# Gate and up products of four feed-forwards as seven block products instead of eight, with weight sums made by VectorE and by accumulating DMAs

## The chip, the cores and the metric

One NeuronCore of one Trainium2 chip. The metric is the device time of the kernel in microseconds (us). The kernel before took 2505.16 us (median of three runs, 2500.97 to 2505.35). TensorE is called PE, VectorE DVE, ScalarE ACT, GpSimd POOL and SyncE SP, as in the profile; PEld is PE's weight load.

## The reference, cut to what matters

A token block `x` of 512 tokens by 1024 features passes a first block (attention, short convolution, an expert feed-forward) and then a second block of two layers. Each layer of the second block holds two dense feed-forwards, so there are four, in this order: before and after a pooling mixer, before and after a latent attention.

```python
D_FF = 2816
FFN_HALF = 0.5

def swiglu(h, w_gate, w_up, w_down):
    return (jax.nn.silu(h @ w_gate) * (h @ w_up)) @ w_down

for i in range(DEPTH_2):
    h = rmsnorm_2(x, ffn1_norm[i])
    x = x + FFN_HALF * swiglu(h, ffn1_w_gate[i], ffn1_w_up[i], ffn1_w_down[i])
    h = rmsnorm_2(x, mix_norm[i])
    ...
    h = rmsnorm_2(x, ffn2_norm[i])
    x = x + FFN_HALF * swiglu(h, ffn2_w_gate[i], ffn2_w_up[i], ffn2_w_down[i])
```

All values are float32. The change touches `h @ w_gate` and `h @ w_up` alone.

## The kernel before

Features lie on the 128 partitions and tokens along the free dimension, so `x` is 8 tiles (`KD`) of 128x512. A feed-forward has 22 inner tiles (`KF`) of 128 features each. For one inner tile the kernel loads a strip of the gate weights and a strip of the up weights (128x1024 each, 512 KB), and later 16 strips of the down weights (128x1408). Each of the 88 gate, 88 up and 64 down strips goes the same way. SP loads it into one of four slots of `stage` (`strip`). ACT copies it as fp32r to `wH` (`hi`, L699). DVE writes what the copy left out to `wL` (`lo`, L1856). PE then makes three products for each 128x128 weight tile (`three`, L1142 to L1144): high by high, high by low and low by high, with the split activations `hH` and `hL`. A gate or up strip is 8 x 3 = 24 matmuls of 512 columns, an inner tile 48 and a pair of inner tiles 96. `wH` and `wL` have two slots, so `hi(n)` waits until strip n-2 has been used.

An inner tile (`inner` in `ffn`) takes two banks of PSUM, and successive tiles alternate between two pairs of banks. DVE multiplies the gate bank by `rstd` into `hraw` (L2355) and the up bank into `gf` (L2358), which frees the banks (`out_taken`). ACT takes silu of `hraw` (L739), DVE multiplies (L2361), ACT copies to `gH` (L742) and DVE writes `gL` (L2364). The normalisation factor `rstd` is made while the first two tiles are multiplied; it is applied to the products, not to their input. The down products read `gH` and `gL`, and DVE adds half of each into `x` (L2406).

Each engine runs its own queue in program order, and semaphores tie them. In each feed-forward DVE's queue is: `lo` of strips 2 and 3, the reciprocal (L1871), `lo` of strip 4, `inner(0)`, `lo` of strip 5, `inner(1)`, and then always two strips and one tile. The mixer of the first layer has products of 256 columns (`token_product`, 96 matmuls by `three`), the only ones in the trace with fp32r operands that read split weights as the moving side at 256 columns.

Of the kernel before, what the change touches and what calls it, by code (L numbers as in the profile page):

```python
# [134 lines left out]
def build(nc, A, out):  # L135
    st = ExitStack()
    with st:
# [22 lines left out]
        hL = place("hL", [P, KD, T], F32R, HL)  # L160
        stage = place("stage", [P, STAGE, WIDE], F32, ST)
        wH = place("wH", [P, 2, WIDE], F32R, WH)
        wL = place("wL", [P, 2, WIDE], F32R, WL)
# [81 lines left out]
        gH = place("gH", [P, KF, T], F32R, G)  # L245
        gL = place("gL", [P, KF, T], F32R, G + KF * TILE)

        tok = place("tok", [P, NB, D], F32, G)
        band = place("band", [P, NBAND], F32, G + 37 * KB)
        zero = place("zero", [1, P + T], F32R, G + 42 * KB)  # L250
        squares2 = place("squares2", [P, KD, T], F32, G + 56 * KB)
# [86 lines left out]
        pos_loaded, angle, sines = sem("pos_loaded"), sem("angle"), sem("sines")  # L338
# [4 lines left out]
        out_stored = sem("out_stored")  # L343
# [4 lines left out]
        NFFN = 2 * KF + 2 * KD  # L348
        POOL = FFN1A + NFFN
        FFN2A = POOL + 4  # L350
        FFN1B = FFN2A + NFFN
        M_IN = FFN1B + NFFN
# [5 lines left out]
        N_STRIPS = FFN2B + NFFN  # L358
        width = [KD * P] * FFN1A
        ffn_width = [KD * P] * (2 * KF) + [WIDE] * (2 * KD)  # L360
        width += ffn_width + [4 * P] * 4 + ffn_width + ffn_width
        width += [KD * P] * 11 + [KQ * P] * 12 + [KD * P] * 2 + [KD * P] * KD + ffn_width
# [3 lines left out]
        T_POOL = T_FFN1A + KF + KD  # L366
        T_FFN2A = T_POOL + KD
        T_FFN1B = T_FFN2A + KF + KD
        T_MIN = T_FFN1B + KF + KD
# [52 lines left out]
        def halves(n):  # L422

            if FFN1A <= n < FFN1A + 2:
                return firstH[:, n - FFN1A, :], firstL[:, n - FFN1A, :]
            return wH[:, n % 2, 0:width[n]], wL[:, n % 2, 0:width[n]]
# [52 lines left out]

        block = st.enter_context(nc.Block())  # L480
# [3 lines left out]
        def _(sp):  # L484
# [19 lines left out]
            def ffn_tiles(n0, f, it):  # L504
                for j in range(2):
                    g = j if it is None else it * 2 + j
                    strip(n0 + 2 * j, A["gate"][f][g], it)
                    strip(n0 + 2 * j + 1, A["up"][f][g], it)

            def ffn(n0, f, start=0):  # L510
                down = A["down"][f]
                with sp.Fori(start, KF // 2) as i:
                    ffn_tiles(n0, f, i)
# [172 lines left out]
        def _(act):  # L686
# [49 lines left out]
            def ffn(n0, t0, f, q):  # L736
# [24 lines left out]
                if f:  # L761
                    hi(n0 + 5)
# [1964 lines left out]
```

## Time and profile before

| what | value |
|---|---|
| three runs | 2505.35, 2500.97, 2505.16 us |
| span of the profiled execution | 2501.0 us |
| PE busy | 2458.6 us, 98% of the span |
| DVE busy | 1132.8 us, 45% |
| ACT busy | 735.2 us, 29% |
| POOL busy | 49.5 us, 2% |
| DMA | 404.29 MB, mean 162 GB/s |
| granted clock of PE | mean 0.994 of full |

The profile has no time of its own for the profiled execution beside its span. The span is 4.2 us below the median of the runs and equal to the fastest of them within 0.1 us.

The feed-forwards lie at 740 to 1124 us, 1149 to 1509 us, 1509 to 1870 us and 2137 to 2501 us. In the profile a matmul's duration overlaps that of the next one, so the pace is read from starts, not from durations.

### The profile page before, as it was taken

The numbers are of one execution on the slowest core, as the hardware profiler recorded it, in microseconds if no ns is written. First come the engines' busy times: TensorE is split into PE (matmuls) and PEld (weight loads), VectorE is DVE, ScalarE is ACT, GpSimd is POOL, SyncE is SP. The second block draws the span as 40 slices with busy tenths as digits, with TensorE's granted clock in tenths as the row PEclk, the third lists the DMA queues.
The fourth block names the chain that finished last, engine by engine and source line by source line (L and its number), as shares of the span: only waits on it lengthen the run. The fifth ranks groups of instructions, "written<-read, shape, count | busy, mean of one in ns | idle before, by whom it ended". The sixth has DMA issues, their size and how long they took to land.

```text
span 2501.0 us, 29717 instructions
## 1 busy us (share of the span) xinstructions
PE 2458.6 (98%) x11265; PEld 1802.0 (72%) x11265; DVE 1132.8 (45%) x1732; ACT 735.2 (29%) x1049; POOL 49.5 (2%) x28
## 2 busy tenths in 40 slices
PE   7999999999999999999999999999999999999999
PEld 4876744434437888888888888888887667888887
DVE  6785312222227444336444334444337565544422
ACT  4245210100014333224333223333224354333321
POOL 0042000000000000000000000000000000000000
PEclk8999999999999999999999999999999999999999
DMA  7552699999992223313222322323222211223332
GB/s 309 191 168 98 262 408 421 421 420 421 421 407 89 98 94 112 102 55 110 92 100 99 104 91 84 101 92 113 96 90 68 80 43 43 93 92 101 105 104 68
DMA packets 84654, 404.29 MB, mean 162 GB/s; under 512 B 9176, under 2 KB 9560, under 8 KB 60896
## 3 DMA queue, kind: packets, MB, share of 16 engines
q1 hardware_dynamic: 84576, 403.22, 43.3%
q8 instruction: 53, 0.87, 0.1%
q14 instruction: 25, 0.20, 0.0%
HBM read 401.08 MB, written 2.10 MB: 161 GB/s over the span
## 4 chain that ended last, share of the span: by engine, by line
PE 92%; DVE 4%; ACT 2%; DMA 1%; issue 1%; SPq 0%; ACTq 0%; DVEq 0%
PE pair L1142 23%; PE pair L1144 23%; PE pair L1143 23%; PE pair L1438 9%; PE pair L1463 4%; PE pair L1374 2%; PE pair L1693 1%; PE pair L1831 1%; PE pair L1402 1%; PE pair L1288 1%; PE pair L1801 1%; PE pair L1802 1%; DMA ada_first<-in_w_ada 1%; PE pair L1403 1%; DMA stage<-in_gate 0%
## 5 line engine op out<-in xcount | busy, mean ns | idle before, releaser
L1856 DVE TENSOR_TENSOR wL<-stage,wH 128x1024 fp32r<-128x1024 f32 (+3 forms) x301 | 389.0, 1292 | 775.0 <-ACT wH L699 774.5
L1142 PE MATMUL pair<-hH,wH 128*128 128x512 f32 x1672 | 658.4, 394 | 8.5 <-DVE hL L1966 2.9
L1144 PE MATMUL pair<-hH,wL 128*128 128x512 f32 x1672 | 651.7, 390 | 0.0
L1143 PE MATMUL pair<-hL,wH 128*128 128x512 f32 x1672 | 651.6, 390 | 0.0
L699 ACT ACTIVATE wH<-stage 128x1024 fp32r<-128x1024 f32 (+3 forms) x301 | 335.2, 1114 | 842.1 <-PE pair L1144 842.1
L1142 PEld LDWEIGHTS pair<-hH,wH 128*128 128x128 f32 x1672 | 314.4, 188 | 80.3 <-DVE hL L1901 4.2
L1143 PEld LDWEIGHTS pair<-hL,wH 128*128 128x128 f32 x1672 | 314.5, 188 | 66.9 <-issue 2.4
L1144 PEld LDWEIGHTS pair<-hH,wL 128*128 128x128 f32 x1672 | 314.4, 188 | 65.8
L1142 PE MATMUL pair<-gH,wH 128*128 128x512 f32 x704 | 273.9, 389 | 0.0
L1143 PE MATMUL pair<-gL,wH 128*128 128x512 f32 x704 | 273.9, 389 | 0.0
L1144 PE MATMUL pair<-gH,wL 128*128 128x512 f32 x704 | 273.9, 389 | 0.0
L1438 PE MATMUL pair<-ring,xsT 128*64 128x512 f32 x1008 | 225.0, 596 | 0.0
L1438 PEld LDWEIGHTS pair<-ring,xsT 128*64 128x64 f32 x1008 | 69.3, 137 | 135.6 <-issue 134.9
L1142 PEld LDWEIGHTS pair<-gH,wH 128*128 128x128 f32 x704 | 132.1, 188 | 27.6
L1144 PEld LDWEIGHTS pair<-gH,wL 128*128 128x128 f32 x704 | 132.1, 188 | 27.5
L1143 PEld LDWEIGHTS pair<-gL,wH 128*128 128x128 f32 x704 | 132.1, 188 | 27.2
L1463 PE MATMUL pair<-ring,hidT 128*64 128x512 f32 x448 | 101.6, 607 | 6.0 <-issue 4.4
L2257 DVE SCALAR_TENSOR_TENSOR x<-pair,mod,x 128x512 f32<-128x512 f32 x64 | 45.5, 747 | 135.7 <-PE pair L1403 135.7
L739 ACT ACTIVATE sg<-hraw 128x512 f32<-128x512 f32 x88 | 55.7, 633 | 167.1 <-DVE hraw L2355 167.1
L2364 DVE TENSOR_TENSOR gL<-gf,gH 128x512 f32 (+1 forms) x88 | 61.0, 693 | 77.5 <-ACT gH L742 77.5
L1463 PEld LDWEIGHTS pair<-ring,hidT 128*64 128x64 f32 x448 | 31.6, 139 | 66.4 <-issue 64.0
L742 ACT ACTIVATE gH<-gf 128x512 f32 (+1 forms) x88 | 55.7, 633 | 76.7 <-DVE gf L2361 76.7
(365 smaller groups left out, 2135.1 us busy)
## 6 DMA issues: line engine op xcount, KB each, us to landing
ring<-in_experts SPq DMA_DIRECT2D x182, 1024.0 KB, 19.5
stage<-in_gate SPq DMA_DIRECT2D x88, 512.0 KB, 3.2
stage<-in_up SPq DMA_DIRECT2D x88, 512.0 KB, 3.2
stage<-in_down SPq DMA_DIRECT2D x64, 704.0 KB, 4.0
adaw<-in_w_ada SPq DMA_DIRECT2D x32, 512.0 KB, 5.2
stage<-in_w_in SPq DMA_DIRECT2D x18, 512.0 KB, 3.7
ring<-in_experts SPq DMA_DIRECT2D x16, 512.0 KB, 11.4
stage<-in_mla_in SPq DMA_DIRECT2D x9, 512.0 KB, 3.3
```

The costliest lines, as they stand in the source:

```text
L699: act.activation(halves(n)[0], stage[:, n % STAGE, 0:width[n]], ACT.Copy).then_inc(strip_hi, 1)
L739: act.activation(sg[:, tile % 2, :], hraw[:, tile % 2, :], ACT.Silu).then_inc(silu_done, 1)
L742: act.activation(dst, gf[:, tile % 2, :], ACT.Copy).then_inc(g_hi, 1)
L1142: pe.matmul(ps, lh, rh, start=first, stop=False)
L1143: pe.matmul(ps, lh, rl, start=False, stop=False)
L1144: return pe.matmul(ps, ll, rh, start=False, stop=last)
L1374: mm = pe.matmul(ps, xt[:, i, k * P:(k + 1) * P], pick[:, i, :], start=(i == 0), stop=(i == NB - 1))
L1438: mm = pe.matmul(pb[2 * g + half][64 * j:64 * j + 64, :], xsT[:, k, 64 * j:64 * j + 64], w[j][:, half * 512:(half + 1) * 512], start=(k == ...
L1463: mm = pe.matmul(pb[4 + half][64 * j:64 * j + 64, :], hidT[:, k, 64 * j:64 * j + 64], w[j][:, half * 512:(half + 1) * 512], start=(k == 0) ...
L1856: dve.tensor_tensor(low, stage[:, n % STAGE, 0:w], high, ALU.subtract).then_inc(strip_lo, 1)
L2257: dve.scalar_tensor_tensor(out=x[:, k, :], in0=pb[7 - k % 2][:, :], scalar=mod[:, 40 + k:41 + k], in1=x[:, k, :], op0=ALU.mult, op1=ALU.ad ...
L2364: dve.tensor_tensor(gL[:, g, :], gf[:, s, :], gH[:, g, :], ALU.subtract).then_inc(g_lo, 1)
```

## The change

`PLAIN = (3, 2, 2, 2)` pairs of inner tiles of the four feed-forwards are made as before. The other `SEVENS = (8, 9, 9, 9)` pairs, 35 in all, are made by block products. For one pair the weights are a 2 x 2 grid of blocks (512 input features by 128 inner features): `a`, `b`, `c`, `d`, for gate and for up. The input is a 2 x 2 grid too (512 features by 256 tokens). Seven sums of weight blocks ("pieces": `a`, `a+c+d`, `c+d`, `a+c`, `b`, `d`, `a+b+c+d`) are multiplied by seven sums of input quarters. A piece is 2 x 4 x 3 = 24 matmuls of 256 columns, so a pair has 168.

The input sums are made once per feed-forward, while the plain tiles run. DVE makes the normalised input (`normalised`, 8 operations of 128x512), four sums (`mix_sums`, 128x1024), and, after a copy by ACT (`mix_out`), seven low parts (`mix_low`, 128x1024). `rstd` is then in the input, not applied afterwards.

The weight sums `c+d` and `a+c+d` are made by DVE (`sum_cd`, `sum_acd`). `a+c` and `a+b+c+d` are made in place by two accumulating DMAs each that POOL issues (`sums_in_place`): `block_a += c`, after DVE has read `a` and made `a+c+d`, and `block_c += b`. Each piece is split by ACT and DVE as a strip was (`piece_high`, `piece_low`), into a ring of three buffers. From PSUM DVE takes the partial results (`take_first`, `take_under`, `take_left`, `take_top`), and ACT keeps the first product (`first_copy`). The rows of the pair are then finished by silu, product and split (`make_*`, `silu_*`, `under_*`, `top_*`).

The input sums need the room of `x`, so `x` is stored to DRAM (`x_kept`, 2 MB) and loaded back before the first down tile is added. All loops over inner tiles are unrolled. The four feed-forwards alternate between a low and an up place of `x`, `hH` and `hL`. In the first of them `norm_sum` and the like stay as they were; in the others `norm_sum` comes one strip earlier on PE.

The core of the diff:

```diff
+        PLAIN = (3, 2, 2, 2)
+            def sums_in_place(f):
+                for p in range(SEVENS[f]):
+                    pool.wait_ge(piece_lo, PIECE0 + piece_count(f, "a", p))
+                    pool.wait_ge(blocks_summed, LOADED0 + 2 * (SEVEN0[f] + p) + 2)
+                    for m in range(2):
+                        pool.dma_start(block_a[:, m, :], block(f, p, 2, m), accum_op=ALU.add).then_inc(a_summed, 16)
+                    pool.wait_ge(piece_lo, PIECE0 + piece_count(f, "ac+d", p))
+                    for m in range(2):
+                        pool.dma_start(block_c[p % 2][:, m, :], block(f, p, 1, m), accum_op=ALU.add).then_inc(c_summed, 16)
...
+            def seventh(f, kind, p, ps, i, first):
+                w = piece_place(f, piece_no(f, kind, p))
+                pe.wait_ge(piece_lo, PIECE0 + piece_count(f, kind, p))
...
+                for m in range(2):
+                    to = ps[:, 512 * m:512 * m + T // 2]
+                    for k in range(KD // 2):
+                        high, low = (w[:, j, m, k * P:(k + 1) * P] for j in range(2))
+                        h = mix[SIDE[f]][:, i, k, :, :]
+                        pe.matmul(to, high, h[:, 0, :], start=first and k == 0, stop=False, skip_group_check=True)
+                        pe.matmul(to, high, h[:, 1, :], start=False, stop=False, skip_group_check=True)
+                        mm = pe.matmul(to, low, h[:, 0, :], start=False, stop=k == KD // 2 - 1, skip_group_check=True)
+                mm.then_inc(piece_used, 1)
...
+                for p in range(SEVENS[f]):
+                    s = SEVEN0[f] + p
+                    if p:
+                        pe.wait_ge(part_taken, PIECE0 + 5 * s - 1)
+                    seventh(f, "ac+d", p, main, T2, True)
...
+                    seventh(f, "c+d", p, side, T1, True)
+                    pe.wait_ge(part_taken, PIECE0 + 5 * s + 1)
+                    seventh(f, "a+c", p, main, T3, False)
+                    pe.wait_ge(first_kept, PIECE0 + s + 1)
+                    seventh(f, "b", p, first, B21, False)
+                    pe.wait_ge(part_taken, PIECE0 + 5 * s + 2)
+                    seventh(f, "d", p, main, T4, False)
+                    pe.wait_ge(part_taken, PIECE0 + 5 * s + 3)
+                    seventh(f, "all", p, side, B22, False)
...
+                for p in range(SEVENS[f]):
+                    more = p + 1 < SEVENS[f]
+                    if p:
+                        make_under(f, p - 1)
+                        make_top(f, p - 1)
+                    piece_low(f, "a+c", p)
+                    take_first(f, p)
...
+                    if more:
+                        sum_cd(f, p + 1)
+                        piece_low(f, "a", p + 1)
+                    take_left(f, p)
+                    if more:
+                        sum_acd(f, p + 1)
+                        piece_low(f, "ac+d", p + 1)
+                    take_top(f, p)
+                    if more:
+                        piece_low(f, "c+d", p + 1)
...
+                for j in range(4):
+                    if (d0 + j) % STAGE == 3:
+                        sp.wait_ge(piece_used, PIECE0 + pieces_end(f) - (2 if ring_turn(f)[0] == 0 else 0))
+                    strip(d0 + j, down[j])
```

The last lines are SP's: the first down strips (`d0` on) wait there where their slot of `stage` overlaps a piece. In the fourth feed-forward that is so for `d0` itself, with a wait for the last piece's products.

**The start of a feed-forward on DVE.** The third one, from the reciprocal on. Before:

```order
L1871 RECIPROCAL rstd<-std 128x512
L1856 TENSOR_TENSOR wL<-stage,wH 128x1024
L2355 TENSOR_TENSOR hraw<-pair,rstd 128x512
L2358 TENSOR_TENSOR gf<-pair,rstd 128x512
L2361 TENSOR_TENSOR gf<-gf,sg 128x512
L2364 TENSOR_TENSOR gL<-gf,gH 128x512
L1856 TENSOR_TENSOR wL<-stage,wH 128x1024
L2355 TENSOR_TENSOR hraw<-pair,rstd 128x512
```

The same place with the change:

```order
L2193 TENSOR_TENSOR wHL<-stage,wHL 128x1024
L2689 SCALAR_TENSOR_TENSOR normal_up<-x_up,cols,rstd 128x512 x8
L2802 TENSOR_TENSOR hraw<-pair,rstd 128x512
L2805 TENSOR_TENSOR gf<-pair,rstd 128x512
L2808 TENSOR_TENSOR gf<-gf,sg 128x512
L2811 TENSOR_TENSOR g_up_157<-gf,g_up_157 128x512
L2193 TENSOR_TENSOR wHL<-stage,wHL 128x1024
L2701 TENSOR_TENSOR mix_raw_up<-normal_up 128x4x256
L2703 TENSOR_TENSOR mix_raw_up<-normal_up,mix_raw_up 128x4x256
L2704 TENSOR_TENSOR mix_raw_up<-normal_up 128x4x256
L2706 TENSOR_TENSOR mix_raw_up<-normal_up,mix_raw_up 128x4x256
L2717 TENSOR_TENSOR mix_up<-normal_up,mix_up 128x4x256
```

Eight operations now stand between the low part of strip 4 and the first read of PSUM, and seven more (with the two that follow these rows) between the low part of strip 5 and `inner(1)`.

**The end of a feed-forward's gate and up on ACT.** The fourth one, from the last inner tile to the first down strips. Before:

```order
L739 ACTIVATE sg<-hraw 128x512
L742 ACTIVATE gH<-gf 128x512
L699 ACTIVATE wH<-stage 128x1408 x2
L739 ACTIVATE sg<-hraw 128x512
L742 ACTIVATE gH<-gf 128x512
```

With the change (`f_row<-top_row` is the silu that needs the last block product):

```order
L957 ACTIVATE piece_180<-block_c_176 128x1024
L971 ACTIVATE f_row<-pair 128x256
L978 ACTIVATE f_row<-under_row 128x512
L983 ACTIVATE f_row<-top_row 128x256
L876 ACTIVATE wHL<-stage 128x1408
L988 ACTIVATE g_low_156<-f_row 128x512
```

The copy of the first down strip stood ahead of the last inner tile's silu; now it stands behind it.

## Rows read from the trace of the kernel before

**Rows 1.** The page, part 1 and PEclk of the 40 slices.

```profile
PE 2458.6 (98%) x11265; PEld 1802.0 (72%) x11265; DVE 1132.8 (45%) x1732; ACT 735.2 (29%) x1049; POOL 49.5 (2%) x28
...
PEclk8999999999999999999999999999999999999999
```

**Rows 2.** The page, part 5, costliest groups: count, busy us, mean ns, idle before.

```profile
L1142 PE MATMUL pair<-hH,wH 128*128 128x512 f32 x1672 | 658.4, 394 | 8.5 <-DVE hL L1966 2.9
```

**Rows 3.** Timeline of DVE, 1527 to 1545 us, third feed-forward: start, duration, instruction.

```profile
1528.34 1.23 DVE L1856 TENSOR_TENSOR wL<-stage,wH 128x1024 fp32r<-128x1024 f32 x1 [1.03 <-ACT wH L699]
1529.48 0.68 DVE L2355 TENSOR_TENSOR hraw<-pair,rstd 128x512 f32<-128x512 f32 x1
1530.08 0.68 DVE L2358 TENSOR_TENSOR gf<-pair,rstd 128x512 f32<-128x512 f32 x1
1530.93 0.69 DVE L2361 TENSOR_TENSOR gf<-gf,sg 128x512 f32<-128x512 f32 x1 [0.17 <-ACT sg L739]
1532.32 0.69 DVE L2364 TENSOR_TENSOR gL<-gf,gH 128x512 fp32r<-128x512 f32 x1 [0.70 <-ACT gH L742]
1533.71 1.22 DVE L1856 TENSOR_TENSOR wL<-stage,wH 128x1024 fp32r<-128x1024 f32 x1 [0.69 <-ACT wH L699]
...
1539.09 1.23 DVE L1856 TENSOR_TENSOR wL<-stage,wH 128x1024 fp32r<-128x1024 f32 x1 [0.70 <-ACT wH L699]
1544.53 1.23 DVE L1856 TENSOR_TENSOR wL<-stage,wH 128x1024 fp32r<-128x1024 f32 x1 [4.21 <-ACT wH L699]
```

**Rows 4.** Timeline of PE in the mixer, first and last of 46 matmuls of 256 columns.

```profile
1124.32 0.28 PE L1144 MATMUL pair<-wH,hL 128*128 128x256 f32 x1
...
1129.72 0.28 PE L1144 MATMUL pair<-wH,hL 128*128 128x256 f32 x1
```

**Rows 5.** Timeline of ACT, 1527 to 1545 us.

```profile
1532.61 1.06 ACT L699 ACTIVATE wH<-stage 128x1024 fp32r<-128x1024 f32 x1 [0.32 <-PE pair L1144]
1535.57 0.63 ACT L739 ACTIVATE sg<-hraw 128x512 f32<-128x512 f32 x1 [1.89 <-DVE hraw L2355]
```

**Rows 6.** DMA issues of the page's part 6 and of the DMA view: count, KB, us to landing.

```profile
stage<-in_gate SPq DMA_DIRECT2D x88, 512.0 KB, 3.2
stage<-in_down SPq DMA_DIRECT2D x64, 704.0 KB, 4.0
...
out<-x SPq DMA_DIRECT2D x8, 256.0 KB, 4.9
stage<-in_pool_w SPq DMA_DIRECT2D x4, 256.0 KB, 2.6
```

**Rows 7.** Timelines of DVE and ACT, first feed-forward, 799 to 815 us.

```profile
799.79 1.23 DVE L1856 TENSOR_TENSOR wL<-stage,wH 128x1024 fp32r<-128x1024 f32 x1 [0.26 <-ACT wH L699]
800.94 2.06 DVE L2346 SCALAR_TENSOR_TENSOR x<-x,cols,pair 128x512 f32<-128x512 f32 x3
...
808.66 1.06 ACT L699 ACTIVATE wH<-stage 128x1024 fp32r<-128x1024 f32 x1 [1.99 <-PE pair L1144]
```

**Rows 8.** Groups by form: the split of a down strip on DVE and on ACT.

```profile
L1856 DVE TENSOR_TENSOR wL<-stage,wH 128x1408 fp32r<-128x1408 f32 x64 | 104.0, 1626 | 274.6 <-ACT wH L699 274.6
...
L699 ACT ACTIVATE wH<-stage 128x1408 fp32r<-128x1408 f32 x64 | 88.4, 1382 | 274.9 <-PE pair L1144 274.9
```

**Rows 9.** Timeline of PE, 48 equal matmuls in two rounds of the expert loop.

```profile
458.02 10.52 PE L1463 MATMUL pair<-ring,hidT 128*64 128x512 f32 x48 [0.25 <-ACT hidT L933]
...
517.95 12.88 PE L1463 MATMUL pair<-ring,hidT 128*64 128x512 f32 x48 [4.39 <-issue]
```

**Rows 10.** Windows of PE: stretch, length, busy (instructions), granted clock, DMA share, GB/s.

```profile
34.00:36.00 2.00, 0.00 (x0) 0.66 1.01 399
36.00:38.00 2.00, 1.86 (x4) 0.50 1.01 406
38.00:40.00 2.00, 2.00 (x6) 0.50 1.04 414
500.00:510.00 10.00, 10.00 (x68) 1.00 1.01 421
510.00:520.00 10.00, 5.61 (x39) 0.80 1.01 416
520.00:530.00 10.00, 10.00 (x42) 0.86 1.02 422
1540.00:1697.00 157.00, 157.00 (x694) 1.00 0.29 97
```

More of the change, by code:

```diff
@@ L502, in strip, with ffn_tile @@
                 sp.dma_start(stage[:, n % STAGE, 0:width[n]], src).then_inc(strip_landed[n % STAGE], 16)
[L504 to L508, printed above, removed]
-            def ffn(n0, f, start=0):
-                down = A["down"][f]
-                with sp.Fori(start, KF // 2) as i:
-                    ffn_tiles(n0, f, i)
-                d0 = n0 + 2 * KF
-                with sp.Fori(0, KD // 2) as i:
+            def ffn_tile(n0, f, tile):
+                strip(n0 + 2 * tile, A["gate"][f][tile])
+                strip(n0 + 2 * tile + 1, A["up"][f][tile])
@@ L682, in _ @@
             pool.memset(kr[:, :, :], 0.0).then_inc(pool_made, 1)
+            sums_in_place(3)
         @block.scalar
@@ L752, in ffn @@
+                    act.activation(g_tile(f, tile)[0], gf[:, tile % 2, :], ACT.Copy).then_inc(g_hi, 1)
                 if f:
@@ L767, in ffn @@
                     hi(n0 + 8)
                     hi(n0 + 9)
[L769 to L773 removed]
+                    for i in MIX_ORDER[0:3]:
+                        mix_out(f, i)
+                    inner(3)
+                    hi(n0 + 10)
+                    hi(n0 + 11)
+                    for i in MIX_ORDER[3:7]:
+                        mix_out(f, i)
@@ L1551, in ffn, with inner @@
             def ffn(n0, t0, f, q):
                 lows = LO0[q]
-                def inner(tile, it, waits):
+                high, low = hHs[SIDE[f]], hLs[SIDE[f]]
+                def inner(tile, waits):
                     for part in range(2):
@@ L1603, in token_product @@
                 half = g // 2
-                high, low = (w[:, (POOL + g) % 2, 0:4 * P].rearrange("p (m k c) -> p m k c", m=2, k=2) for w in (wH, wL))
+                high, low = (wHL[:, (POOL + g) % 2, i, 0:4 * P].rearrange("p (m k c) -> p m k c", m=2, k=2) for i in range(2))
                 pe.wait_ge(strip_lo, POOL + g + 1)
@@ L2379, in ffn @@
                     lo(n0 + 4)
-                inner(0, None)
-                lo(n0 + (5 if f else 6))
-                inner(1, None)
-                if f == 0:
-                    lo(n0 + 7)
+                    for k in range(KD):
+                        normalised(f, q, k)
+                    inner(0)
+                    lo(n0 + 5)
+                    mix_sums(f)
+                    for i in MIX_ORDER[0:3]:
+                        mix_low(f, i)
+                    inner(1)
+                    lo(n0 + 6)
@@ L2385, in ffn @@
+                    lo(n0 + 7)
+                    for i in MIX_ORDER[3:7]:
+                        mix_low(f, i)
+                    inner(2)
+                else:
+                    inner(0)
+                    lo(n0 + 6)
+                    inner(1)
+                    lo(n0 + 7)
+                    for k in range(KD):
+                        normalised(f, q, k)
                     for k in range(3):
                         normed(k)
-                    inner(2, None)
+                    inner(2)
```

536 lines of the change are left out of this document (437 added, 99 removed).

## Prediction

> **What bounds the kernel now.** I read the page's busy times first: PE is busy 98% of the span, DVE 45%, ACT 29%, and the granted clock is at its upper level (2.4 GHz) in nearly every slice [rows 1]. The costliest group of matmuls, 658 us, waited 8.5 us in all [rows 2]. In the plain part of a feed-forward PE has no gap (157.00 us busy of 157.00) [rows 10]. So a microsecond of PE work saved there is saved in the span, as long as DVE and ACT deliver. DVE waits for ACT, and ACT for PE to free a slot [rows 3, 5]: both have room now. The question is what they have left when PE gets faster and they get more work.
>
> **PE's work.** Two splits of gate and up strips start 5.44 us apart (1539.09 and 1544.53) [rows 3]. A strip is 24 matmuls, so one of 512 columns takes 0.2267 us, and a pair of inner tiles 96 x 0.2267 = 21.76 us. The nearest row for the new form is the mixer's: 45 matmuls of 256 columns from 1124.32 to 1129.72, 0.120 us each [rows 4], with the same three products and a weight load for each. Half the columns so cost 53% of the time, not half. A pair of seven products is 168 x 0.120 = 20.16 us (2.88 us for a piece), 1.60 us less; 12.5% fewer columns become 7.4% less time. 35 pairs save 56.0 us. This is the whole gain.
>
> **Steady pairs: does DVE keep up?** Prices from starts: 1024 elements 1.14 us (1528.34 to 1529.48), with the result there after 1.23; 512 elements 0.60 (1529.48 to 1530.08) [rows 3]. By this slope 256 elements take 0.33, an estimate. A pair needs nine operations of 1024 (seven low parts, two sums), eight of 512, two of 256: 10.3 + 4.8 + 0.7 = 15.8 us of 20.16. ACT needs seven of 1024 at 1.06 and four of 512 at 0.63 [rows 5] and two smaller: about 10.8. Both fit, if the order does. I walked one pair, t = 0 being PE's start on `a+c+d`, pieces every 2.88. Product `b` ends at 11.7, so silu and `make_corner` end at 12.7, and `sum_cd` for the next pair ends at 13.8, low part of `a` at 14.9. `take_left` needs product `d` (14.6) and ends at 15.6, `sum_acd` at 16.7; ACT's copy 17.8; low part of `a+c+d` 19.1, wanted at 20.2. `c+d` is ready at 20.9, wanted at 23.0. Every piece is at least 1 us early. I take no stall, provided the DMAs are in time.
>
> Loads: a pair still loads 2 MB, in halves of 256 KB. Block `d` is asked for at 8.3 and wanted at 12.7. One 256 KB load lands in 2.6 us, and twice the bytes in 3.2 [rows 6], so two land in about 3.5 with the second's issue. That fits. POOL's accumulating DMAs (1 MB more per pair) have no row. `block_a += c` is issued at 16.7. After it come ACT's copy and DVE's low part and `take_first` (1.1 + 1.2 + 0.7, with waits 3.1 us), and PE wants the result at 25.9. So both DMAs may take **6.1 us** before PE waits. Lower end: two plain loads, 3.5. Upper end: an accumulation is a load and a store one after the other, 2.6 + 4.9 + 0.6 = 8.1 [rows 6]. I take 4 to 5, nearer to the loads, since bytes and target are those of the loads and the store row's target is DRAM; it costs nothing below 6.1. The Trainium skill ("DMA: Bandwidth & Descriptors", Anatomy of one DMA) gives an issue from GpSimd 2.0 us plus bytes at 436 GB/s. Its page "SBUF — State Buffer" (Who interferes with whom) speaks against the change: DVE operations with both inputs in SBUF contend with GpSimd's reads, and most of DVE's new work is of that kind. No row of before shows either.
>
> **The start of a feed-forward.** DVE gets 8 + 4 + 7 operations that come before PE's next needs. Prices: a 512-element operation with a scalar and two tensors takes 0.66 (three in about 2.0) [rows 7], so `normalised` is 5.3 us; the eleven of 1024 are 12.5 us. In the third feed-forward strips 2 and 3 end at 1532.6 [rows 5]. Before, `gf` freed the banks at 1530.8 [rows 3]. Now DVE does low part 4 (to 1529.5), eight `normalised` (to 1534.8), `hraw`, `gf` (to 1536.1): PE waits **3.5 us**. Then, rest of `inner(0)` 2.3, low part 5 1.2, four sums 4.6, three low parts 3.4, `inner(1)` 3.5, and only then ACT's copy 6 and low part 6: ready at 1553.1, where PE would have ended the third tile's strips at 1547.0: **6.1 us**. Then low parts 7 and four more (5.7), `inner(2)` (3.5), `sum_cd`, `sum_acd` and the low part of `a` (3.5): ready at 1565.8, where PE ends at 1564.0: **1.8 us**. PE begins the block products 11.5 us later than without a wait (1554.3 by 21.76 from 1532.6). It is a matter of totals: DVE's queue from 1528.3 to there holds 37 us, and PE's work ends after 26.
>
> The clock adds to it. After a gap of 4.39 us the same 48 matmuls took 12.88 instead of 10.52 us [rows 9], and the granted clock was 0.80 and 0.86 over the two windows [rows 10]; a gap near 35 us brought it to 0.50, the lower level of 1.2 GHz [rows 10]. So a gap of that size costs 2.4 us more. In the gaps above, the first lies inside DVE's chain, the second partly so: the start is at 1566.4, **12.1 us** late. Second and fourth feed-forward have the same queue: 3 x 12.1 = 36.3.
>
> The first feed-forward has six plain tiles. From 800.94 DVE does eight `normalised` (5.3), three old ones (2.0) [rows 7], `inner(2)` up to `gf`; strip 8 is ready at 813.4 where PE wanted it at 808.6, when strip 7 was used [rows 7]. Later, sums, `inner(3)`, strips 10 and 11, seven low parts, `inner(4)`, two sums and the low part of `a` end at 843.7, where 830.4 was due (four strips after 808.6): 13.2, and 2.4 for the clock: **15.6 us**.
>
> **The end.** Before, the first down strip was split while the last tile ran. Now `take_top` waits for the last product (0.9 with the wait), ACT's `silu_top` (0.4) waits for it, and behind stand the copy of the down strip, 1.38, and its low part, 1.63 [rows 8]: **4.45 us** with the waits between, and 2.4 for the clock, 6.85. In the fourth feed-forward the load itself waits for the last product: 4.0 us to landing [rows 6], then 1.38 and 1.63 and 0.7 of waits and issue: 7.7, with the clock 10.1. Sum 3 x 6.85 + 10.1 = 30.7. The store and reload of `x` (2 MB, some 6 us by the 512 KB row's slope) lie beside PE's first down tile (15 us): nothing. The longer queues of instructions: nothing, PE waited for none in its straight stretches.
>
> **Sum.** 15.6 + 36.3 + 30.7 = 82.6 lost, 56.0 won: +26.6 us on the span of 2501.0, 2527.6. The span lies 4.2 us under the median of the runs; I carry the difference over: 2505.2 + 26.6 = **2531.8 us**.
>
> **Rivals.**
> 1. *Late accumulations.* `block_a += c` takes the upper end, 8.1 us. PE then waits 2.0 us in each pair but the first of a feed-forward (31): +62, 2594 us. For it: no row shows such a DMA, and POOL must write its descriptors beside a DVE that is busy three quarters of the time. Against: the loads in this stretch land in 3.2 us and the DMA engines are 29% busy [rows 10]. Its point is 6.1 us; each microsecond beyond is 31 us. Chance 0.30.
> 2. *Faster on the other side: weights used twice are cheap.* 512 columns less 256 is 0.2267 - 0.120 = 0.1067 us for 256 columns, so 13.3 ns of each matmul is not columns. If that part falls away in block products, where two successive matmuls have the same weights, a pair is 168 x 0.1067 = 17.9 us, DVE still just keeps up, and 35 pairs save 134 instead of 56: 2454 us. It decides at 0.1155 us a matmul, where the gain becomes the losses. Against: the mixer's rows have the same repeated weights and show 0.120. The Trainium skill ("TensorE: Matmul & The Clock Gate", Back-to-back issue gap) has 262 cycles, 0.109 us, for 256 columns; by it the gain is 120 and the time 2468. The rows speak against it already at 512 (0.2267 measured). Chance 0.06.
> 3. *The clock stays up.* The gaps are shorter than computed or the clock does not fall: without its 14 us it is 2518 us. Against: rows 10. Chance 0.10.
> 4. *The start is mostly hidden.* If DVE's operations of 4 x 256 elements between SBUF operands run well above the rate of the flat ones, the start costs half, 26 less, and with a better clock the sum is near zero: 2505 or a little less. No row shows such operands. Chance 0.10.
> 5. The forecast itself, within some 10 us: 0.44.
>
> The change does what it says as far as the order of the queues shows: there is no case for "nothing changed".
>
> **Chances and range.** No change means within 0.2% (5 us), about what a measurement of this kernel can tell. Faster: rival 2, part of 4, and something unforeseen: 0.12. Same: the rest of 4: 0.06. Slower: 0.82. The range goes from 2508, which leaves out the faster cases, to 2598, just above the upper end for the DMAs.
>
> **What would show it.** Matmuls of 256 columns in the feed-forwards 0.120 us apart; in the third feed-forward PE idle about 3.5, 4 to 6 and up to 2 us before the first block product, released by DVE; PE idle 4.4 us (fourth: 7.7) before the first down strip; granted clock under 1.00 right after. In steady pairs PE without gaps, DVE about 78% busy. I am wrong if PE waits in every pair behind `a+c` (late accumulations), if the pace differs from 0.120, or if the starts cost under 5 us each.

## The result, and the profile after

The changed kernel took 2588.9 us (median of four runs, 2587.11 to 2592.31); the kernel before, on the same chip, 2504.5 us (2500.97 to 2505.35). The ratio is 1.034, with a 95% interval of 1.0326 to 1.0355. The forecast was 2531.8 us: slower as expected, and inside the range, but by 84 us instead of 27.

The first lines of the page after, to be read against [rows 1]: PE has 9 us less busy time, and the span grew by 85, so PE's idle time grew by 95 us. The matmuls' work was to fall by 56 us: the other 47 are time that matmuls behind gaps took more (14 of them the forecast had in its clock terms). DVE has 285 us more work and is at 55% instead of 45%.

```profile
span 2586.4 us, 34667 instructions
...
PE 2449.2 (95%) x13785; PEld 1903.2 (74%) x13785; DVE 1418.2 (55%) x2053; ACT 869.3 (34%) x1252; POOL 172.7 (7%) x168
...
q0 software_dynamic: 20160, 36.71, 9.0%
...
PE 62%; DVE 16%; DMA 12%; issue 5%; ACT 4%; SPq 1%; POOL 1%; DVEq 0%; POOLq 0%; ACTq 0%
```

The last line is the chain that ended last: 12% of it are DMAs and 16% DVE, although PE is busy 95% of the span. The waits of PE say where (engine and line, what was waited for: us in total, times, longest):

```profile
PE pair L1435 <- DVE wHL L2193: 39.4, 10, 7.5
PE pair L1855 <- DVE top_row L2746: 34.6, 33, 2.8
PE pair L1435 <- DVE gf L2805: 11.9, 4, 4.0
```

The first and third line are mainly the starts and ends of the feed-forwards. The second one was not in the forecast: L2746 is `take_first`, and the waiting instruction is the first matmul of the piece `a+c`, in nearly every pair.

**Starts and ends as forecast.** The timeline of PE in the third feed-forward (start, duration, instruction, idle before it and its releaser):

```profile
1583.00 0.47 PE L1435 MATMUL pair<-hH_up,wHL 128*128 128x512 f32 x1 [3.98 <-DVE gf L2805]
1599.83 0.79 PE L1435 MATMUL pair<-hH_up,wHL 128*128 128x512 f32 x1 [4.09 <-DVE wHL L2193]
1622.15 0.38 PE L1855 MATMUL pair<-mix_up,piece_up 128*128 128x256 f32 x1 [0.20 <-DVE top_row L2746]
```

The third gap, of up to 2 us, that the forecast had ahead of the block products did not come in the last three feed-forwards. The distance from the end of the first gap to the first `a+c` is 39.15 us; the forecast's is 38.9 (start of the block products at 1566.4, three pieces of 2.88 later 1575.0, less 1536.1). So the total was right, though it came in fewer gaps. In the first feed-forward PE waited 5.61, 1.31 and 5.19 us, 12.1 in all, where 13.2 was forecast. The ends show 4.34 us in the first and third feed-forward, 4.49 in the second and 7.45 in the fourth, where 4.45 and 7.7 were forecast. After each such gap the granted clock falls (stretch, length, busy, clock, DMA share, GB/s):

```profile
1024.00:1028.00 4.00, 3.97 (x11) 0.57 0.98 410
1600.00:1604.00 4.00, 4.00 (x10) 0.50 0.48 141
```

**The steady pairs not as forecast.** From the first `a+c` of the third feed-forward (1622.15 us) to the ninth (1796.84) are 8 pairs of 21.84 us; 20.16 was forecast. Over all 31 intervals between pairs the mean is 21.71 us (from the starts of `sum_cd`). 35 x 1.55 = 54 us, nearly all of the missing 57. One pair's chain, in order of time (start, us, what):

```profile
1666.09 1.36 SPq L627
...
1667.49 0.43 SPq L639
...
1667.97 3.58 DMA block_d<-in_up
...
1671.64 1.22 DVE block_e L2725
...
1673.92 0.68 DVE under_row L2759
1674.60 1.14 DVE block_c L2731
...
1676.28 0.54 POOL block_a L843
1676.81 5.67 DMA block_a<-in_up
...
1682.51 1.07 ACT piece L957
...
1684.74 0.68 DVE top_row L2746
```

The reader is to see a loop that PE's work hardly enters: SP issues the loads of block `d` (L639) as soon as DVE's low part of the last `d` has freed the block, `d` lands, `sum_cd` and `sum_acd` follow on DVE, POOL issues the two accumulating DMAs, and the second lands 5.67 us after its issue. Then come ACT's copy, DVE's low part and `take_first`. Behind them DVE makes the low parts of `b` and `d`, which frees block `d` for the next load: the loop is closed.

The issue of `b` that took 1.36 us is the longest of 35, whose median is 0.43. It ended 0.02 us after the low part of `d`, so it cost nothing. In 30 of the 31 pairs `load_d` follows that low part within 0.06 us.

The steps of this pair, from PE's first `a+c` on: 3.5 us to the load of `d`, 4.15 until `sum_cd` starts, 4.1 for DVE up to the end of `sum_acd`, 6.8 to ACT's copy, 3.0 to the next `a+c`: 21.46 us. From the end of `sum_acd` to ACT's copy are 6.8 us here (1675.74 to 1682.51). Over the 31 pairs that are not the first of a feed-forward, this stretch (read in each pair from the timelines of DVE and ACT) has a mean of 7.0 us and lies between 6.1 and 8.6.

The page's DMA issues answer to [rows 6] (count, KB, us from issue to landing):

```profile
block_d<-in_gate SPq DMA_DIRECT2D x35, 256.0 KB, 3.2
block_d<-in_up SPq DMA_DIRECT2D x35, 256.0 KB, 3.7
block_a<-in_gate SPq DMA_DIRECT2D x35, 256.0 KB, 2.6
block_a<-in_up SPq DMA_DIRECT2D x35, 256.0 KB, 2.9
...
block_a<-in_gate POOLq DMA_DIRECT2D x35, 256.0 KB, 4.0
block_a<-in_up POOLq DMA_DIRECT2D x35, 256.0 KB, 5.8
```

And where the wait is long the clock goes down too. Two steady pairs of the second feed-forward, one quiet and the last one:

```profile
1243.09:1263.80 20.71, 20.41 (x168) 1.00 0.64 153
...
1393.73:1417.99 24.26, 23.12 (x169) 0.87 0.49 110
...
1393.73 0.58 PE L1855 MATMUL pair<-mix_low,piece 128*128 128x256 f32 x1 [2.82 <-DVE top_row L2746]
1394.12 0.42 PE L1856 MATMUL pair<-mix_low,piece 128*128 128x256 f32 x1
1394.33 0.41 PE L1857 MATMUL pair<-mix_low,piece 128*128 128x256 f32 x1
```

After the gap of 2.82 us the matmuls start 0.21 us apart instead of 0.12. This is not the rule. Of the 37 waits in the block products only four had such a stretch behind them, after gaps of 1.73, 1.86, 1.95 and 2.82 us, some 7 us of loss together. After one of 1.92 us the clock stayed up:

```profile
1007.92:1011.92 4.00, 4.00 (x33) 1.00 0.00 0
1730.10:1734.10 4.00, 4.00 (x22) 0.62 0.72 220
```

Every wait costs something else too. The first matmul behind it starts 0.28 us plus the idle time after the last one, and the second 0.22 us later, where 0.12 is the pace: 0.26 us a time, some 9 us in all, which the profile counts as busy.

### The profile page after: what moved, and what is told of

It is laid out like the page before. It is cut to its first block, busy times and chain, and to the rows that moved or that the text cites. A ratio compares the mean times of both kernels' runs of the same rounds, so it can differ in the third digit from the quotient of the medians.

```text
span 2586.4 us, 34667 instructions
## 1 busy us (share of the span) xinstructions
PE 2449.2 (95%) x13785; PEld 1903.2 (74%) x13785; DVE 1418.2 (55%) x2053; ACT 869.3 (34%) x1252; POOL 172.7 (7%) x168
## 4 chain that ended last, share of the span: by engine, by line
PE 62%; DVE 16%; DMA 12%; issue 5%; ACT 4%; SPq 1%; POOL 1%; DVEq 0%; POOLq 0%; ACTq 0%
PE pair L1435 11%; PE pair L1436 11%; PE pair L1437 11%; PE pair L1731 9%; DMA block_a<-in_up 7%; PE pair L1756 4%; DMA block_d<-in_up 3%; DVE piece L2738 2%; PE pair L1667 2%; PE pair L1855 2%; PE pair L1856 2%; PE pair L1857 2%; DVE block_e L2725 1%; DVE block_c L2731 1%; DVE wHL L2193 1%
## 5 line engine op out<-in xcount | busy, mean ns | idle before, releaser
L2193 DVE TENSOR_TENSOR wHL<-stage,wHL 128x1024 fp32r<-128x1024 f32 (+3 forms) x161 | 217.0, 1350 | 438.4 <-ACT wHL L876 438.2
L1855 PE MATMUL pair<-mix_low,piece 128*128 128x256 f32 x1392 | 399.4, 287 | 25.5 <-DVE top_row L2746 24.9
L1856 PE MATMUL pair<-mix_low,piece 128*128 128x256 f32 x1392 | 396.5, 285 | 0.0
L1857 PE MATMUL pair<-mix_low,piece 128*128 128x256 f32 x1392 | 396.3, 285 | 0.0
L876 ACT ACTIVATE wHL<-stage 128x1024 fp32r<-128x1024 f32 (+3 forms) x161 | 185.9, 1157 | 507.0 <-PE pair L1437 502.5
L1855 PEld LDWEIGHTS pair<-mix_low,piece 128*128 128x128 f32 x1392 | 269.7, 194 | 30.9 <-DVE top_row L2746 29.5
L1857 PEld LDWEIGHTS pair<-mix_low,piece 128*128 128x128 f32 x1392 | 269.9, 194 | 0.0
L1856 PEld LDWEIGHTS pair<-mix_low,piece 128*128 128x128 f32 x1392 | 269.8, 194 | 0.0
L1435 PE MATMUL pair<-hH,wHL 128*128 128x512 f32 x488 | 203.8, 418 | 29.4 <-DVE wHL L2193 14.7
L1435 PE MATMUL pair<-g_low,wHL 128*128 128x512 f32 x528 | 207.8, 394 | 16.3 <-DVE wHL L2193 16.3
L1437 PE MATMUL pair<-g_low,wHL 128*128 128x512 f32 x528 | 207.1, 392 | 0.0
L1436 PE MATMUL pair<-g_low,wHL 128*128 128x512 f32 x528 | 207.0, 392 | 0.0
L1436 PE MATMUL pair<-hL,wHL 128*128 128x512 f32 x488 | 196.3, 402 | 0.0
L1437 PE MATMUL pair<-hH,wHL 128*128 128x512 f32 x488 | 195.9, 401 | 0.0
L1855 PE MATMUL pair<-mix_up,piece 128*128 128x256 f32 x480 | 137.4, 286 | 9.6 <-DVE top_row L2746 8.6
L957 ACT ACTIVATE piece<-block_c 128x1024 fp32r<-128x1024 f32 x66 | 70.0, 1060 | 208.6 <-DVE block_c L2731 122.9
L1435 PEld LDWEIGHTS pair<-hH,wHL 128*128 128x128 f32 x488 | 95.5, 196 | 57.9 <-DVE wHL L2193 17.7
L1856 PE MATMUL pair<-mix_up,piece 128*128 128x256 f32 x480 | 136.6, 284 | 0.0
L1857 PE MATMUL pair<-mix_up,piece 128*128 128x256 f32 x480 | 136.5, 284 | 0.0
```

The source lines that it names most:

```text
L876: act.activation(halves(n)[0], stage[:, n % STAGE, 0:width[n]], ACT.Copy).then_inc(strip_hi, 1)
L957: act.activation(piece_place(f, i)[:, 0, :, :], src[:, :, :], ACT.Copy).then_inc(piece_hi, 1)
L1435: pe.matmul(ps, lh, rh, start=first, stop=False)
L1436: pe.matmul(ps, lh, rl, start=False, stop=False)
L1437: return pe.matmul(ps, ll, rh, start=False, stop=last)
L1855: pe.matmul(to, high, h[:, 0, :], start=first and k == 0, stop=False, skip_group_check=True)
```

## The experiments

The theory (A): the pair is a loop through the sum on DVE, the accumulating DMA and ACT's copy, and only its latency counts. Rivals: DVE's amount of work is the bound (B), memory traffic slows everything (C), the two accumulations of a pair crowd one queue (D). All times are medians; the kernel before took 2502.6 to 2503.0 us beside them. A pair's period is read from the starts of one DVE sum, pair after pair.

**1. Without `block_a += c`.**

```diff
-                    for m in range(2):
-                        pool.dma_start(block_a[:, m, :], block(f, p, 2, m), accum_op=ALU.add).then_inc(a_summed, 16)
```

> Leaves out the two accumulating DMAs of block_a += c in every pair, so the piece a+c is a alone (its product is another number; all other work stays). Theory A (the changed kernel's steady pair of 21.84 us is a loop through DVE's sum, this DMA and ACT's copy): PE's wait ahead of a+c (about 1.0 us a pair, plus the clock it costs) goes away, the pair falls to 20.4 us, 35 pairs give 44 to 50 us: 2539 to 2545 us. Theory B (the pair is bound by DVE's amount of work, whatever the DMA does): no more than 10 us less, 2579 or more. Theory C (the accumulations slow everything through the shared SBUF): nearly as A, but the starts and the DVE operations become shorter too.

Measured: 2534.3 us, ratio 1.0129 (1.0112 to 1.0146), 54.6 us less. The 31 intervals between pairs add up to 624.6 us, 20.15 each, which is the forecast's 168 x 0.120 (with the accumulation they were 673.0, 21.71 each). (ACT's wait for the sum goes with the DMAs.) PE's waits on L2746 are gone; its busy time fell as well, from 2449.2 to 2429.9 us, with the same number of matmuls. So the 55 us are 34.6 us of waits and 19.3 us of time that counts as busy: some 9 of it the 0.26 us at each wait, some 7 the four stretches at the lower clock, the rest not told apart. C falls: the low part of `d` takes 1226 ns here and 1221 before, and the gaps of the starts are as long (11.6 us behind `gf`, against 11.9). B is not yet excluded, since nothing was added to DVE. Nor is the traffic of these DMAs, which went with them (experiment 6 keeps it).

**2. Without `block_c += b`.**

```diff
-                    for m in range(2):
-                        pool.dma_start(block_c[p % 2][:, m, :], block(f, p, 1, m), accum_op=ALU.add).then_inc(c_summed, 16)
```

> Leaves out the two accumulating DMAs of block_c += b in every pair, so the last piece is a+c+d without b. Theory A (only block_a += c lies in the loop): within 10 us of 2589, since the wait ahead of a+c stays, and block_a += c still lands 5.5 to 6 us after its issue. Theory D (the two accumulations crowd one queue, and the a-sum is late because of the c-sum of the same or the previous pair): block_a += c lands in 4.5 us or less and the time falls by 20 us or more, to 2569 or less.

Measured: 2579.0 us, ratio 1.0305 (1.0286 to 1.0324), 10 us less, just at A's edge. `block_a += c` still lands 5.6 us after its issue, the stretch from sum to copy has a mean of 6.8 us. D falls: the second accumulation adds little to the first.

**3. `a+c` by VectorE.** The accumulating DMAs of `a` go, and DVE gets a third sum of 1024 elements a pair.

```diff
-                dve.tensor_tensor(block_c[p % 2][:, :, :], block_e[:, :, :], block_a[:, :, :], ALU.add).then_inc(blocks_summed, 1)
+                dve.tensor_tensor(block_a[:, :, :], block_a[:, :, :], block_c[p % 2][:, :, :], ALU.add).then_inc(blocks_summed, 1)
+                dve.wait_ge(blocks_summed, LOADED0 + 3 * (SEVEN0[f] + p) + 2)
+                dve.tensor_tensor(block_c[p % 2][:, :, :], block_a[:, :, :], block_d[:, :, :], ALU.add).then_inc(blocks_summed, 1)
```

> a+c is made by VectorE in block_a once a has been split, and a+c+d from it; three sums of 1024 elements a pair by VectorE instead of two, and only block_c += b stays a DMA. Same values up to rounding. Theory A (DMA in the loop): the pair falls to about 20.4 us although VectorE has 1.14 us more to do (about 17 of 20.4 us): 2539 to 2552 us. Theory B (VectorE's amount bounds): the time rises above 2589, by up to 35 x 1.14 = 40 us.

Measured: 2560.2 us, ratio 1.0233 (1.0216 to 1.025). With 40 us more work DVE made the kernel 29 us faster, so B falls. Most pairs take 20.39 us, A's number; some take up to 22.06, 5 us in all. The time is 8 us above A's range. Missed was the first pair of each feed-forward, 22.1 to 24.1 us (11 us over the four): three sums now stand ahead of the last plain tile on DVE, and the low part of `c+d` behind it; in the fourth feed-forward PE waited 1.85 us there.

**4. `take_left` behind `sum_acd`.**

```diff
-                    take_left(f, p)
                     if more:
                         sum_acd(f, p + 1)
+                    take_left(f, p)
+                    if more:
                         piece_low(f, "ac+d", p + 1)
```

> In VectorE's queue sum_acd comes before take_left instead of behind it; nothing else changes. In the loop of the changed kernel take_left with its wait for PE stands for 0.6 to 1.1 us between the low part of a and sum_acd. Theory A: the loop gets shorter by that, the pair falls to 20.7 to 21.2 us, 30 pairs give 18 to 34 us: 2555 to 2571 us. Theory B (amount of work): within 5 us of 2589.

Measured: 2572.9 us, ratio 1.0282 (1.0265 to 1.0299): 16 us from exchanging two entries of a queue, 2 us less than the least that A expected and more than B allows. DVE's wait for block `d` stays in the loop (20.9 us in 25 pairs; 19.4 in 26 before the exchange).

**5. The low part of `a` first.**

```diff
                     if more:
-                        sum_cd(f, p + 1)
                         piece_low(f, "a", p + 1)
-                    take_left(f, p)
-                    if more:
+                        sum_cd(f, p + 1)
                         sum_acd(f, p + 1)
+                    take_left(f, p)
+                    if more:
                         piece_low(f, "ac+d", p + 1)
```

> VectorE's queue alone is reordered: the low part of a, then sum_cd, sum_acd, and take_left behind them (it was sum_cd, low part of a, take_left, sum_acd). No operation or DMA goes. The sum a+c+d then ends one low part (1.14 us) after the landing of block d less, and take_left's wait lies behind it: some 1.7 us earlier in the loop. Theory A (the pair of 21.84 us is that loop, and nothing in PE, DVE or the DMAs is short of rate): the pair falls to 20.16 us, as without block_a += c, 35 pairs give 45 to 55 us, 2534 to 2544 us. Theory E (what no_a_sum won came from less traffic or less contention, not from the wait): no more than left_later won, 2570 us or more.

Measured: 2571.5 us, ratio 1.0268 (1.0248 to 1.0288). A missed this one by 27 us. DVE's wait for `d` is gone (0.9 us in all), and still no more was won than by experiment 4. The timelines of DVE and ACT show why:

```profile
2303.28 0.42 DVE L2771 TENSOR_TENSOR f_row<-pair,f_row 128x256 f32<-128x256 f32 x1 [0.74 <-ACT f_row L971]
2304.22 1.23 DVE L2738 TENSOR_TENSOR piece<-block_a,piece 128x1024 fp32r<-128x1024 f32 x1 [0.52 <-ACT piece L957]
2305.37 1.22 DVE L2725 TENSOR_TENSOR block_e<-block_c,block_d 128x1024 f32<-128x1024 f32 x1
2306.69 1.23 DVE L2731 TENSOR_TENSOR block_c<-block_e,block_a 128x1024 f32<-128x1024 f32 x1
...
2302.86 0.38 ACT L971 ACTIVATE f_row<-pair 128x256 f32<-128x256 f32 x1 [1.75 <-PE pair L1857]
2303.14 1.05 ACT L957 ACTIVATE piece<-block_a 128x1024 fp32r<-128x1024 f32 x1
2307.95 1.06 ACT L957 ACTIVATE piece<-block_c 128x1024 fp32r<-128x1024 f32 x1 [3.76 <-DVE block_c L2731]
...
2314.49 1.06 ACT L957 ACTIVATE piece<-block_a 128x1024 fp32r<-128x1024 f32 x1 [2.39 <-DMA block_a<-in_up]
```

ACT's copy of the next `a` waits in its queue behind the silu that needs product `b`, so the low part of `a` can't start before PE is through with `b`. The sum then ends at 2307.92. Counted from the product's end (2302.86, which the prediction's walk had at 11.7) this is 16.8 us into the pair, where the walk had 16.7. From here ACT waits 6.57 us. In this kernel the prediction's schedule is met, and the wait of PE is what the DMA takes above the 6.1 us that the prediction had allowed it; over the 31 pairs that mean is 7.0 us (6.1 to 8.7). In the longest one POOL's second issue came 1.79 us after the first instead of 0.54, with nothing in the profile that it waited for. PE's gap there was 2.38 us, and the clock was 0.59 for 4.1 us behind it. This late issue is no chance event: in all seven kernels of this case in which POOL issues four DMAs a pair it is between the 113th and the 114th of them (1.8 us), at 2260 to 2338 us of the span.

**6. A plain write instead of an accumulation.**

```diff
-                        pool.dma_start(block_a[:, m, :], block(f, p, 2, m), accum_op=ALU.add).then_inc(a_summed, 16)
+                        pool.dma_start(block_a[:, m, :], block(f, p, 2, m)).then_inc(a_summed, 16)
```

> The two DMAs of block_a += c stay in POOL's queue, at the same place, but write c over a without adding (so the piece a+c is c alone). It measures what adding costs by itself. If the 5.8 us from issue to landing belong to POOL's queue (descriptors written by POOL, one queue for both halves), it lands in 5 to 5.8 us and the time stays within 10 us of 2589. If they belong to the adding (a read and a write of SBUF), it lands in 3 to 3.6 us like SP's loads, some 2.3 us earlier, PE's wait ahead of a+c goes, and the time is that of no_a_sum, 2532 to 2542 us.

Measured: 2533.5 us, ratio 1.0123 (1.0108 to 1.0139). The DMA issues of this kernel:

```profile
block_a<-in_gate POOLq DMA_DIRECT2D x35, 256.0 KB, 2.9
block_a<-in_up POOLq DMA_DIRECT2D x35, 256.0 KB, 3.1
block_c<-in_gate POOLq DMA_DIRECT2D x35, 256.0 KB, 4.1
block_c<-in_up POOLq DMA_DIRECT2D x35, 256.0 KB, 5.6
```

The last two rows were these before, behind two adding DMAs:

```profile
block_c<-in_gate POOLq DMA_DIRECT2D x35, 256.0 KB, 5.7
block_c<-in_up POOLq DMA_DIRECT2D x35, 256.0 KB, 6.7
```

Same engine, queue, bytes and place in the program: without the addition the second half lands in 3.1 us instead of 5.8. From the end of the sum to ACT's copy the mean is 4.4 us instead of 7.0. `block_c += b`, which still adds, now takes what `block_a += c` took, 4.1 and 5.6. The cost belongs to the adding, not to POOL's queue, and not to DVE's accesses alone, which are the same in both. No run has an adding DMA beside an idle DVE, so whether adding suffers more from them is not shown.

**7. All sums of `a`, `c` and `d` by VectorE, in a better order** (low part of `a`, `a+c`, `a+c+d`, `take_left`, `c+d`).

```diff
+                dve.tensor_tensor(block_a[:, :, :], block_a[:, :, :], block_c[p % 2][:, :, :], ALU.add).then_inc(blocks_summed, 1)
...
+                dve.tensor_tensor(block_e[:, :, :], block_a[:, :, :], block_d[:, :, :], ALU.add).then_inc(blocks_summed, 1)
...
+                dve.tensor_tensor(block_c[p % 2][:, :, :], block_c[p % 2][:, :, :], block_d[:, :, :], ALU.add).then_inc(blocks_summed, 1)
```

> VectorE makes a+c (in block_a), then a+c+d (in block_e) and c+d (in block_c), in the order low part of a, a+c, a+c+d, take_left, c+d; only a+b+c+d stays with the accumulating DMA. Against ac_by_dve (2560 us, pair 20.39 us, late by the low part of a+c+d) block d is wanted 2.3 us later and the sum a+c+d ends 1 to 1.7 us earlier. Theory A (only waits kept the pair above 20.16 us): the pair falls to 20.16 us with VectorE at 17 us of work in it, and the time to that of no_a_sum, 2534 us, or 2532 to 2542 us. Theory B (with three sums VectorE is at its limit): 2555 us or more.

Measured: 2544.8 us, ratio 1.0169 (1.0153 to 1.0184). Every steady pair is 20.16 us within 0.02, but for one of 20.51, with ten operations of 1024 elements on DVE in it. The time is 3 us above A's end: the first pairs take 21.6 to 23.1 us.

**8. The first down strip ahead of `silu_top` and `take_top`.**

```diff
+                lo(d0)
+                take_top(f, SEVENS[f] - 1)
```

> In the last pair of a feed-forward ScalarE copies the first down strip ahead of silu_top, and VectorE makes its low part ahead of take_top; only the order changes. In the first three feed-forwards the copy and low part (3.0 us) then lie beside the last block product (2.9 us): the gaps of 4.3 to 4.5 us ahead of the down products nearly vanish, and with them the lower clock behind them (2.0 to 2.4 us each): 18 to 20 us less, 2569 to 2571 us. In the fourth the load waits for the last product, so its gap of 7.45 us stays within 1 us. If the gap is due to something else (the load of the strip, the row of g): within 5 us of 2589.

Measured: 2575.1 us, ratio 1.0286 (1.0269 to 1.0303), 14 us less. The time is 4 us above the expectation. (In ACT's queue `silu_top` moves behind the copy in the same way.) The gaps of 4.3 to 4.5 us became 1.7 to 1.9, not zero: ACT had `silu_under` to do ahead of the copy. The fourth, behind the load, stayed at 7.3 us, as expected. Behind them the clock stays up. The second row is from a steady pair of this kernel, behind a gap of 2.77 us:

```profile
1023.45:1027.45 4.00, 4.00 (x18) 1.00 1.09 441
...
1746.85:1750.85 4.00, 4.00 (x33) 1.00 0.70 241
```

Three times 2.65 us of gap are 8 of the 14 us. In the 4 us behind such a gap 18 matmuls start instead of 11, which is 1.6 us of work, or 5 us for the three. That the clock accounts for the whole rest is not shown: the two profiled executions are only 9.1 us apart.

**9. One more plain pair in feed-forwards two to four, with the input sums spread over it.**

```diff
-        PLAIN = (3, 2, 2, 2)
+        PLAIN = (3, 3, 3, 3)
```

> PLAIN = (3, 3, 3, 3): one more plain pair in feed-forwards two to four, and the 19 extra VectorE operations and ScalarE copies of the start spread between the strips of all six plain tiles instead of four. By my account the start of each of these cost 12.1 us (queue 37 us against 26 of PE's work, and the clock); with another 21.8 us of PE's work it is hidden but for 1 to 2 us: 3 x 10 to 3 x 12 us less. Three pairs cost 21.76 instead of 21.84 us: nothing. 2552 to 2560 us. If the starts cost little and the loss is elsewhere: 2580 us or more.

Measured: 2564.9 us, ratio 1.0254 (1.0237 to 1.0271), 24 us less. The gaps of 4.0 and 4.1 us are gone; there remain 1.05 us ahead of strip 6 and 2.1 to 2.6 us ahead of the block products, where the first blocks are only loaded once the last strip has been split. The time is 5 to 13 us above the expectation. The gaps are read from the fastest of its four runs (2556.4 us; the others took 2563.7 to 2569.1), so they do not explain that miss.

**10. The three changes of order together** (5, 8 and 9).

> The three changes of order together (a_first, early_down, spread_start). If the causes are separate and add up: 32 pairs at 20.16 us give 45 to 50 us, the ends 19, the starts 30 to 36, less three pairs that are plain at 21.76 instead of 20.16 us (5): 2589 - 89 to 2589 - 100, 2489 to 2500 us, as fast as the kernel before or up to 0.6% faster. If one delay stands in for another, 2515 us or more.

Measured: 2533.8 us, ratio 1.0124 (1.0107 to 1.0141). The three gains measured singly were 17, 14 and 24 us, together 55: so they add up. The time lies in the range set for "one delay stands in for another" (2515 or more), but not for that reason: it is 34 us above the expectation, and the three single times lay 27, 4 and 5 us above theirs.

**11. A version from what was learnt** (7, 8 and 9, a fourth plain pair in the first feed-forward, and `a` loaded first).

> dve_sums, early_down and spread_start together, and two things more: the first feed-forward gets a fourth plain pair, with its 19 operations spread between the strips (the split of its tiles 4 and 5 waits until the input sums are done), and at the start of the block products a is loaded first and its low part made first (all_three lost 2.6 us there in each feed-forward). From all_three (2534 us): 28 steady pairs at 20.16 instead of 21.24 us give 30, the starts of the block products 10, the start of the first feed-forward 11 less 1.6 for the plain pair: 2475 to 2495 us, 0.3 to 1.1% under the kernel before. If the pairs stay above 20.8 us, 2500 us or more.

Measured: 2501.2 us, ratio 0.999 (0.9981 to 0.9999), 6 us above the range. All steady pairs are at 20.16 us; in the first pair of a feed-forward PE still waited some 3 us, most of it for the `c+d` piece, which stood behind the last plain tile.

**12. The same with four moves in the order.** Shown is the one for the `c+d` piece. The others load `a` one strip earlier, put two of the `normalised` operations behind the low part of strip 6, and put off work between the tiles of the first feed-forward. How much each brought was not measured.

```diff
-                inner(2 * PLAIN[f] - 1)
                 piece_low(f, "c+d", 0)
+                inner(2 * PLAIN[f] - 1)
```

> best with four more moves in the order, no other work: at the start of the block products a is loaded one strip earlier; the c+d piece of the first pair is made ahead of the last plain tile; two of the normalised operations go behind the low part of strip 6; in the first feed-forward the operations between tiles 2 and 6 are put off until the low parts of strips 8 to 15 are in time. In best PE waited there 1.1 to 1.7, 2.1, 1.4 and in the first feed-forward 0.9 and 2.7 us, 18 us over the four, and some lower clock behind it. If these waits go: 2480 to 2490 us, 0.5 to 0.9% under the kernel before. If DVE's queue only moves the waits elsewhere: 2495 us or more.

Measured: 2489.8 us (2487.16 to 2490.34), ratio 0.9946 (0.9933 to 0.996): 13 us less than the kernel before, half a per cent, and 11 us less than experiment 11, which only drew level. Five runs lie within 3.2 us, all below every run of the kernel before (2500.42 us and up). Its page and a stretch of seven pairs:

```profile
span 2485.4 us, 33896 instructions
...
PE 2416.6 (97%) x13497; PEld 1869.2 (75%) x13497; DVE 1433.0 (58%) x2056; ACT 861.2 (35%) x1232; POOL 104.2 (4%) x90
...
1216.00:1358.00 142.00, 140.50 (x1168) 1.00 0.49 128
```

## Why the prediction was off, point by point

1. *What bounds the kernel* held: PE's time, as long as the others deliver.
2. *PE's work*, 0.120 us a matmul and 20.16 us a pair: exact, once nothing waits (experiments 1, 6, 7, 12). The mixer's 46 matmuls [rows 4] were the right price. Rival 2 (weights used twice are cheap) fell.
3. *DVE keeps up*: right in the amount of work. It has room even for a third sum (experiment 7). The walk's times were met when the low part of `a` stands first (experiment 5).
4. *`block_a += c` takes 4 to 5 us*: **this step failed.** What it measured is 7.0 us from the sum to ACT's copy (mean of 31). Of this 1.1 us pass until POOL's second issue, and some 5.8 until it lands; the walk had room for 6.1 in all. I had placed it near the loads [rows 6], because bytes and target are theirs; experiment 6 shows that without the adding this would have been right (3.1 us to landing, 4.4 us from sum to copy). My upper end of 8.1 us, a read and a write one after the other, was the nearer one. So it was rival 1 that happened, at 7.0 instead of 8.1 us, and its total came out nearly as priced (2594 forecast, 2588.9 measured) by luck. By its own rule, 31 us for each microsecond above 6.1, 7.0 us cost 28; the kernel lost 54. The rest has two reasons that rival 1 did not name:
   - Block `d` does not fit ("That fits"), and **this was the second wrong step**: the walk went through one pair with fixed times and did not carry a late `a+c` into the next. `load_d` comes 3.5 us after PE's `a+c`, behind the low parts of `b` and `d`. With `a+c` on PE at 5.8, just in time, that is 9.3 on the walk's clock, not 8.3. `sum_cd` starts 4.4 us after the load's issue (mean of 31; the halves land in 3.2 and 3.7, the second issued 0.4 later), so at 13.7 instead of 12.7. With the 0.9 us of the DMA above its 6.1 this makes a pair longer by nearly 2 us, where 1.55 were measured. Experiment 4 won 16 us by taking `take_left` out of the loop, experiment 5 no more by taking out the wait for `d` as well, because ACT's copy of `a` came in its place.
   - Each wait cost 0.26 us beside its length, and behind four of them the clock fell. I had counted the clock for the starts and ends, and nothing for the pairs. This is some 16 of the 55 us.
5. *The starts*, 15.6 and 12.1 us, and *the ends*, 6.85 and 10.1: right. The gaps at the ends were met within 0.3 us. With plain writes in place of the accumulation the kernel took 2533.5 us, 30.7 more than the kernel before beside it, where the forecast had 26.6 more. So all terms but the one for the steady pairs were right together within 4 us.
6. The contention rule cited from the Trainium skill ("SBUF — State Buffer", Who interferes with whom) is not what made the DMA late: with DVE's work unchanged the plain write landed in 3.1 us (experiment 6). I had read too much into it: the same section says that `tensor_tensor`, the form of all these sums and low parts, did not stall DMAs in the probe it reports.

What stays open: why two accumulations of 256 KB in one queue land 4.0 and 5.8 us after issue where plain writes take 2.9 and 3.1, and why the 114th of POOL's DMAs was issued 1.3 us late in seven kernels. Neither was tried apart.

## What to carry to other kernels

Where a queue of steps closes on itself from one round to the next, add up the latencies round the loop as well as each engine's work: here every engine had room, and the loop of 21.7 us still set the pace. Go round it more than once: a time by which one step is late comes back through everything that waits for it, here the load of `d`. A DMA that adds is not priced like a DMA that writes; if the sum is on a path, an engine with room makes it in 1.2 us. Fewer matmul columns only pay when the start and the end of each stretch are ordered as carefully as its middle: the order of the queues (with three more plain pairs to spread the start over) was worth 55 us here (experiment 10), the seven products themselves 56 (35 pairs at 1.60).

## What the runs showed that I had not expected

- An accumulating DMA of 256 KB took 4.0 us to landing, and its follower in the same queue 5.8; without the addition 2.9 and 3.1.
- Gaps of much the same length were followed by different clocks. Behind gaps of 4.0 to 4.5 us in the changed kernel it was 0.50 to 0.66 over the next 4 us. Gaps of 1.73, 2.4 (experiment 5) and 2.8 us had 4 to 6 us of matmuls 0.21 us apart behind them, while one of 1.92 and one of 2.77 us (experiment 8) had none, nor had the three of 1.7 to 1.9 us at the ends in experiment 8. What makes the difference was not tried.
- The 114th of POOL's DMAs was issued late in seven kernels, whether they added or only wrote.
